# Two transformer blocks on one core: the last four expert output matrices loaded and multiplied by row halves in place of column halves

## What is computed

```python
# first block, end: 32 experts, each token goes to 2 of them
hdn = lax.ragged_dot(xs, w_e_in, group_sizes)        # w_e_in:  32 x 1024 x 512
gate_h, up_h = jnp.split(hdn, 2, axis=-1)
act = jax.nn.silu(gate_h) * up_h                     # 256 wide
ys = lax.ragged_dot(act, w_e_out, group_sizes)       # w_e_out: 32 x 256 x 1024
ys = ys * gates.reshape(-1)[order][:, None]
h = h + jnp.zeros_like(xt).at[tok_sorted].add(ys)
h = rms_norm(h, norm_f_g)
# second block begins: h2 = rmsnorm(h, ln1_2); z = h2 @ w_in_2 ...
```

## Time and profile before

| | |
|---|---|
| median of three runs | 881.14 us (880.82 to 881.31) |
| the profiled execution | 881.2 us, its span 879.5 us |
| TensorE busy | 817.6 us, 93% of the span |
| VectorE, ScalarE, GpSimd busy | 500.8, 374.7, 93.8 us |
| mean granted TensorE clock | 0.981 of full speed |
| DMA | 217.46 MB, mean 247 GB/s over the span |
| experts | about 290 to 488 us of the span |

### The profile page before, as it was taken

One profiled execution on the slowest core, in us unless ns is written; L12 is line 12 of the kernel. 1 busy time (PEld: TensorE's weight loads), 2 busy tenths in 40 slices (PEclk: granted clock), 3 DMA queues, 4 the chain that ended last, 5 costly groups with the idle time before them and its releaser, 6 DMA issues.

```text
span 879.5 us, 13309 instructions
## 1 busy us (share of the span) xinstructions
PE 817.6 (93%) x5226; PEld 650.2 (74%) x5227; DVE 500.8 (57%) x781; ACT 374.7 (43%) x532; POOL 93.8 (11%) x116
## 2 busy tenths in 40 slices
PE   5999999999999997696698999999999999999997
PEld 5998789878888443331232899777778999999995
DVE  5998577865573321111110777466676787776865
ACT  5433644555343301001021755546544755554632
POOL 4132000231000000000000201212260100000000
PEclk9999999999999999897899999999999999999999
DMA  9666365254989999999999994443727756555311
GB/s 293 231 208 239 143 240 193 93 173 143 384 292 390 414 422 423 422 420 421 423 423 399 304 220 175 178 147 141 192 97 241 262 186 217 170 186 184 106 49 48
DMA packets 95434, 217.46 MB, mean 247 GB/s; under 512 B 14047, under 2 KB 44893, under 8 KB 83609
## 3 DMA queue, kind: packets, MB, share of 16 engines
q1 hardware_dynamic: 94697, 215.06, 68.0%
q10 hardware_dynamic: 576, 1.44, 0.5%
q0 software_dynamic: 112, 0.30, 0.1%
HBM read 215.44 MB, written 1.34 MB: 246 GB/s over the span
## 4 chain that ended last, share of the span: by engine, by line
PE 70%; DMA 13%; DVE 8%; ACT 3%; issue 2%; SPq 2%; POOL 1%; DVEq 0%; POOLq 0%; ACTq 0%
PE ps L978 15%; PE ps L980 15%; PE ps L979 15%; DMA moe_ring<-in_w_expert_in 10%; PE ps L1546 7%; PE ps L1421 5%; PE ps L1037 2%; SPq L845 1%; DMA up_odd_d<-in_w_expert_out 1%; PE ps L1386 1%; DVE w_lo L1991 1%; PE ps L1043 1%; DMA stage_b<-in_w_up 1%; PE ps L1447 1%; PE ps L1441 1%
## 5 line engine op out<-in xcount | busy, mean ns | idle before, releaser
L1991 DVE TENSOR_TENSOR w_lo<-stage,w_hi 128x2048 fp32r<-128x2048 f32 (+1 forms) x44 | 95.8, 2216 | 26.4 <-ACT w_hi L1633 24.4
L1633 ACT ACTIVATE w_hi<-stage 128x2048 fp32r<-128x2048 f32 (+1 forms) x44 | 79.4, 1852 | 44.1 <-PE ps L980 26.6
L979 PE MATMUL ps<-w_lo,x_hi 128*128 128x512 f32 (+1 forms) x232 | 88.7, 382 | 0.0
L978 PE MATMUL ps<-w_hi,x_hi 128*128 128x512 f32 x152 | 61.0, 402 | 0.0
L980 PE MATMUL ps<-w_hi,x_lo 128*128 128x512 f32 x152 | 59.3, 390 | 0.0
L1421 PE MATMUL ps<-moe_ring,qk 128*32 128x512 f32 x304 | 48.2, 687 | 10.6 <-DMA moe_ring<-in_w_expert_in 10.6
L980 PE MATMUL ps<-x_hi,w_lo 128*128 128x256 f32 x192 | 54.3, 283 | 0.0
L979 PEld LDWEIGHTS ps<-w_lo,x_hi 128*128 128x128 f32 x232 | 43.7, 188 | 7.9
L980 PE MATMUL ps<-f_hi,w_odd 128*128 128x256 f32 x160 | 45.3, 283 | 0.0
L979 PE MATMUL ps<-f_lo,w_lo 128*128 128x256 f32 x160 | 45.3, 283 | 0.0
L979 PE MATMUL ps<-f_lo,w_odd 128*128 128x256 f32 x160 | 45.3, 283 | 0.0
(11 more groups left out here) (437 smaller groups left out, 2272.1 us busy)
## 6 DMA issues: line engine op xcount, KB each, us to landing
stage<-in_w_in SPq DMA_DIRECT2D x22, 2048.0 KB, 8.1
moe_ring<-in_w_expert_in SPq DMA_DIRECT2D x38, 1024.0 KB, 17.5
moe_ring<-in_w_expert_out SPq DMA_DIRECT2D x16, 1024.0 KB, 17.0
stage_b<-in_w_up SPq DMA_DIRECT2D x12, 1024.0 KB, 7.3
stage<-in_w_down SPq DMA_DIRECT2D x11, 1024.0 KB, 4.9
stage<-in_w_up SPq DMA_DIRECT2D x10, 1024.0 KB, 7.6
up_odd<-in_w_expert_in SPq DMA_DIRECT2D x8, 1024.0 KB, 17.7
down_odd_a<-in_w_expert_out SPq DMA_DIRECT2D x6, 1024.0 KB, 23.1
```

The costliest lines, as they stand in the source:

```text
L978: mm(out, still[0], moving[0], start=first, stop=False)
L979: mm(out, still[0], moving[1], start=False, stop=False)
L1633: act(split_pair(n)[0][:, cols], staged(n)[:, cols], ACT.Copy).then_inc(hi_ready, 1)
L1991: tt(lo[:, cols], staged(n)[:, cols], hi[:, cols].bitcast(fp32), ALU.subtract).then_inc(lo_ready, 1)
```

## The change

```diff
@@ load_rest (SP's queue), the last quad's output matrices
-                for half in range(2):
+                for f in range(2):
                     for j in range(QUAD):
-                        cols = slice(half * BANK, (half + 1) * BANK)
                         e = QUADS * QUAD - QUAD + j
-                        eng.dma_start(expert_down(1, j, True)[:, :, cols], w_down[:, e, :, cols]).then_inc(down_last_in[half], 16)
+                        eng.dma_start(expert_down(1, j, True)[:, f, :], w_down[:, e, f, :]).then_inc(down_last_in[f], 16)
@@ quad (TensorE)
-                def down(half):
-                    for f in range(2):
+                def down(half, rows=range(2)):
+                    for f in rows:
                         for j in range(QUAD):
                             last = mm(ps[CAP * j:CAP * (j + 1), half, :], act_feat[:, f, CAP * j:CAP * (j + 1)],
                                       expert_down(p, j, final)[:, f, half * BANK:(half + 1) * BANK], start=(f == 0), stop=(f == 1),
                                       skip_group_check=True)
-                    last.then_inc((down_a, down_b)[half], 1)
+                    if 1 in rows:
+                        last.then_inc((down_a, down_b)[half], 1)
@@ the last quad's end
                 if final:
                     eng.wait_ge(spread_ready, it + 1)
+                    for f in range(2):
+                        eng.wait_ge(down_last_in[f], r * 64 + 64)
+                        for half in range(2):
+                            down(half, range(f, f + 1))
                     for half in range(2):
-                        eng.wait_ge(down_last_in[half], r * 64 + 64)
-                        down(half)
                         eng.wait_ge((y_a, y_b)[half], it + 2)
                         for t in range(NT):
                             scatter(t, half).then_inc((scat0, scattered)[t] if half == 1 else left_scat, 1)
```

## The result

The changed kernel takes 883.1 us, the median of 20 runs (881.01 to 885.06), beside 881.35 us (880.82 to 882.82, 20 runs) for the kernel before. The ratio is 1.0016, with a 95% interval of 1.0010 to 1.0023. The change makes the kernel slower by about 1.4 us; the medians lie 1.75 us apart. Forecast were 881.4 us and a range from 880.5 to 882.6. The measured time lies above it, at the rival whose mechanism was TensorE's clock (883.1 us).

A forecast was written before the change was run, and what follows sets the result against it. The prediction took the chain through the last loads' landing, set by DMA bytes and rate, to bound the seam. Loads -0.56, hidden copy -0.89 and uncovered scatters +1.75 gave +0.30 us: 881.4 us, range 880.5 to 882.6.

The forecast's parts named there:

- the rival whose mechanism was TensorE's clock: Clock falls in the new 2.7 us gap at the seam, costing 1.7 us: sum +2.0, 883.1 us; chance 0.07.
- the one on TensorE before the last landing: TensorE does 16 records from 478.12 to 480.09, then idles 2.7 us until 482.82, said to cost nothing in itself.
- The sum: At raw_hi: -0.56 loads, -0.89 copy hidden, +1.75 scatters uncovered = +0.30 us, and as much at the kernel's end.
- The sign named for this case: Profile sign that the forecast is wrong in the clock: a granted clock below 1.0 between 482.8 and 489.
- The loads: Last quad's 4.19 MB in 1024 packets of 4 KB, before 2048 of 2 KB: last landing 483.34 to 482.78, 0.56 us saved.
- the line between the two sizes: Cost per packet (8.8 ns) and per byte, from stretches of mostly 8 KB and 2 KB packets; gives 0.56 us saved.
- fixed overhead of about 3 cycles per packet: Skill page's packet cost for the last quad's loads: a saving of 0.24 us in place of 0.56; not used.
- 2 KiB per partition as the least transfer that saturates: Skill's support for the rival that larger rows bring nothing: landing stays at 483.34, sum +0.86, 882.0 us; chance 0.20.
- The cover after the landing: ScalarE's copy hidden by 0.1 us, VectorE's behind half 0's scatters; scatters start 1.85 us after the products, gaining 0.89 us.
- the two uncovered scatters: Half 0's scatters, before covered by TensorE's gap, now follow the last landing: four take 3.73 us, two 1.98; loss 1.75.
- one to one: The chain runs through the seam to TensorE at 519.86, so a delay of raw_hi delays the whole kernel equally.

The follow-up runs named there:

- columns and late scatters: The kernel before, with column loads and column products kept, but all four scatters moved to the end: 883.73 us, ratio 1.0021.
- five filling products: The changed kernel plus five products into an unread PSUM bank after the products with rows f = 0: 881.54 us, ratio 0.9999.
- with three: The changed kernel plus three products into an unread PSUM bank after the products with rows f = 0: 881.81 us, ratio 0.9999.

## Why the prediction was wrong, point by point

**The step that failed** is the one on TensorE before the last landing: 2.7 us idle, and "This costs nothing in itself". The sum had no term for the clock; the runs show one of 1.65 us. The idle time itself was seen, and roughly sized (2.16 and 3.11 us in the two traces), and so was its price, in the rival: 1.7 us forecast from the earlier trace rows. What was wrong was its chance, 0.07. The argument against it was that TensorE works nearly all the time around the gap. In all four traces with an idle time of 2.05 us or more at this place the clock fell, and in none with 1.18 us or less. The rows available ended at 1.38 on one side and 3.73 on the other; 2.7 us in the middle was no reason for one chance in fourteen. The sign named for this case, a granted clock below 1.0 between 482.8 and 489, is the one that came.

Nor would a threshold between 1.18 and 2.05 us be right. Elsewhere in these traces the clock stayed at 1.00 behind idle times of 1.71, 1.91 and 2.07 us between 709 and 714 us, and once behind 3.68 us in the experts, where the nine other traces show a fall behind 3.73 to 4.09 us. What decides beside the length is not shown by any run here.

**The loads: right in the rate.** From 474 to 482 us the packets of 4 KB moved at 409 GB/s, those of 2 KB at 389. The DMA views of the changed kernel and of the one with columns and late scatters:

```profile
DMA packets 913, 3.27 MB, mean 409 GB/s; under 512 B 103, under 2 KB 119, under 8 KB 913
```

```profile
DMA packets 1571, 3.11 MB, mean 389 GB/s; under 512 B 96, under 2 KB 96, under 8 KB 1570
```

For 4.19 MB that is 10.25 in place of 10.77 us, a saving of 0.52 where the line between the two sizes gave 0.56. The Trainium skill's fixed overhead of about 3 cycles per packet ("DMA: Bandwidth & Descriptors", "Why small descriptors are slow (HBM only)") gave an estimate of 0.24, less than the traces show. Its 2 KiB per partition as the least transfer that saturates (same page, "Why a DMA increments its semaphore by 16 and not by 1") was read in the prediction as speaking of the pieces; but it counts what a DMA moves per partition, and that is 4 KB in both kernels, so these runs don't test it. The landing itself varies between executions: 482.80 to 483.40 with rows (four traces with idle time ahead of it), 483.34 and 483.68 with columns. So of the 0.56 us forecast 0.32 showed in the first pair of traces; one landing for each trace can't tell it more exactly.

**The cover after the landing: right.** Without the fall (five filling products) the scatters start 1.86 us after the products, where 1.85 was forecast: ScalarE's copy did not delay them, and VectorE's copy left the path. The sum of both with the two uncovered scatters was forecast at +0.86 us and measured at 0.83.

**The sum** with the clock's term is -0.32 + 0.83 + 1.65 = +2.16 us at `raw_hi` in the profiled pair, all of it explained. The prediction took a delay of `raw_hi` for a delay of the kernel, "one to one". That held as far as 520 us (2.14) and no further: at 711 us 1.76 us are left, and 1.7 at the end. The place is a split of weights on ScalarE (`w_odd`), with the product of TensorE that comes to wait for it. Before:

```profile
697.25 1.91 ACT L1834 ACTIVATE w_odd<-stage_b 128x2048 fp32r<-128x2048 f32 x1 [2.17 <-DMA stage_b<-in_w_up]
...
709.19 0.47 PE L1546 MATMUL ps<-down_hi,act_hi 128*128 128x512 f32 x1 [0.83 <-DVE act_lo L2461]
```

and in the changed kernel:

```profile
699.01 1.92 ACT L1836 ACTIVATE w_odd<-stage_b 128x2048 fp32r<-128x2048 f32 x1 [1.80 <-PE ps L1519]
...
710.95 0.47 PE L1548 MATMUL ps<-down_hi,act_hi 128*128 128x512 f32 x1 [0.46 <-DVE act_lo L2463]
```

Before, ScalarE stood 0.37 us longer, for a load, and TensorE stood 0.37 us longer behind it. In the changed kernel the load is there in time. A load that comes at its own time hides a part of a delay ahead of it, and the ten traces fit that, though not alone. In five the split waits for TensorE, and TensorE's idle time is 0.46 us; there `raw_hi` started at 489.79 or later. In the other five it waits for the load, 2.17 to 3.42 us in place of 1.80, and TensorE's idle time grows by as much, to 0.83 to 2.07 us; four of these have the earliest `raw_hi` (488.80 to 489.50), but the fifth has the latest (columns with late scatters, 491.60), so the load's own time varies as well. With five filling products TensorE stands 1.22 us there, which makes their 0.39 us of delay at 520 into 0.77 at 710.

At the end the 20 runs of each kernel show about 1.4 us (1.75 between the medians) of the 2.16. The load may hide a part of the delay in most executions, and in some the clock may have stayed: 4 of the 20 runs of the changed kernel lie below 882 us. How much each gives is not shown; all four profiles of kernels with a long gap show the fall. That the median is the rival's 883.1 us to the digit is luck in part: the rival was 881.14 + 2.0, and the measured pair is 881.35 + 1.75.

**No version run here is faster than the kernel before.** Without the fall the change still loses 0.83 us of cover for 0.52 us of loading, +0.3 us, and its time isn't told from before. Before, ScalarE was idle for just 0.21 us ahead of `raw_hi`, so a seam with row loads and no scatters left uncovered would probably wait for ScalarE's line 1641 soon; it was not run.

## What to carry to other kernels

When a change takes work out of a wait and puts it behind it, two things are lost: the cover, and the work that kept TensorE busy during the wait. Look in the trace for the idle times of TensorE that did and didn't cost clock, and give a new one in between at least even chances; the price is in the rows behind an old one. Don't take the length for a rule: 2.05 us cost clock at one place and 2.07 us didn't at another. To prove such a case, measure the distance between two events of the seam in the traces, not only the kernel's time: here that distance told 1.65 us with a spread of 0.02, while whole executions spread by up to 4 us.

## What the runs showed of the hardware

At this seam the clock's fall had one price, 1.63 to 1.65 us, for idle times from 2.05 to 3.60 us. Only its place moved: behind 3.60 us the first record was slow (1.07 us), behind 2.05 us the first twelve were hardly slower and the scatters were. In the experts it cost more once: behind 6.83 us of idle time 32 records took 6.43 us in place of 3.64. The same length did not always bring a fall: 2.07 us ahead of 711 us and, in one trace of ten, 3.68 us in the experts left the clock at 1.00. Five products that nobody reads, 2.42 us in all, kept the clock at full speed; with three, 1.18 us of idle time remained and it stayed there too. Packets of 4 KB moved at 408 to 411 GB/s in five traces, those of 2 KB at 388 or 389 in five.
